# Differential attention: a head's output norm in steps among the next head's projections, with two buffers of attended values

## The reference

```python
def _diff_attend(q, k, v, lam):
    s = jnp.einsum('bqhte,bkhte->bhtqk', q, k).astype(jnp.float32) * (q.shape[-1] ** -0.5)
    p = jax.nn.softmax(s, axis=-1)
    a = (p[:, :, 0] - lam * p[:, :, 1]).astype(v.dtype)
    return jnp.einsum('bhqk,bkhe->bqhe', a, v)
...
    yb = _sweep_query_blocks(lambda n, qn: _diff_attend(qn, kb_all, vb_all, lam), qb)
    yb = rmsnorm(yb, b_subln_g) * (1.0 - lam_init)
    y = jnp.concatenate([ya.reshape(B, S, -1), yb.reshape(B, S, -1)], axis=-1) * jax.nn.silu(g)
    x = x + gate * (y @ w_out)
```

## Time and profile before

| what | us |
|---|---|
| median of 3 runs | 3795.56 |
| lowest, highest | 3795.41, 3795.64 |
| the profiled execution's own time | 3793.61 |
| its span, first to last instruction | 3791.6 |
| TensorE busy in the span | 3455.3 (91%) |
| VectorE busy | 2125.5 (56%) |
| ScalarE busy | 1412.0 (37%) |
| GpSimd busy | 298.5 (8%) |

### The profile page before, as it was taken

The page is one execution under the profiler, slowest core; times in us unless marked ns, Lnnn a source line. Parts: engine busy times, 40 slices in busy tenths (PEclk is TensorE's granted clock), DMA queues, the critical chain, the costliest instruction groups (busy, mean ns, idle before and its releaser), DMA issues. The chain is left out here.

```text
span 3791.6 us, 43707 instructions
## 1 busy us (share of the span) xinstructions
PE 3455.3 (91%) x17694; PEld 2681.2 (71%) x17694; DVE 2125.5 (56%) x3914; ACT 1412.0 (37%) x2577; POOL 298.5 (8%) x433
## 2 busy tenths in 40 slices
PE   6999988997998999999899988888799999988888
PEld 4777766664877888887765677777687666676677
DVE  5799954444757666565556554454355444334444
ACT  4222264444133222322333244444324555434441
POOL 2022110001102000000000000000001000000000
PEclk9899998998999999999999998998799999999999
DMA  3333320002522222332210100001212011010112
GB/s 133 111 124 133 139 85 24 23 30 105 190 90 67 81 84 84 111 131 81 84 31 25 49 23 30 23 30 37 97 57 74 30 37 33 23 35 7 35 51 88
DMA packets 76920, 258.21 MB, mean 68 GB/s; under 512 B 9960, under 2 KB 12008, under 8 KB 76720
## 3 DMA queue, kind: packets, MB, share of 16 engines
q1 hardware_dynamic: 42192, 132.68, 10.5%
q0 software_dynamic: 31072, 110.16, 8.5%
q10 hardware_dynamic: 3456, 12.58, 0.8%
HBM read 194.06 MB, written 50.85 MB: 65 GB/s over the span
## 5 line engine op out<-in xcount | busy, mean ns | idle before, releaser
L2878 PE MATMUL PS<-m,m 128*128 128x512 f32 (+3 forms) x3476 | 1394.3, 403 | 92.7 <-DVE m L3238 23.3
L2880 PE MATMUL PS<-m,m 128*128 128x512 f32 (+3 forms) x3476 | 1338.0, 386 | 0.0
L2879 PE MATMUL PS<-m,m 128*128 128x512 f32 (+3 forms) x3476 | 1338.0, 386 | 0.0
L2878 PEld LDWEIGHTS PS<-m,m 128*128 128x128 f32 (+2 forms) x3476 | 664.1, 192 | 325.7 <-issue 73.1
L2880 PEld LDWEIGHTS PS<-m,m 128*128 128x128 f32 (+2 forms) x3476 | 664.6, 192 | 133.7 <-issue 1.0
L2879 PEld LDWEIGHTS PS<-m,m 128*128 128x128 f32 (+2 forms) x3476 | 667.6, 193 | 119.5 <-issue 1.2
L3167 ACT COPY m<-PS 128x512 f32<-128x512 f32 x352 | 205.2, 588 | 451.0 <-PE PS L2994 450.1
L3004 PE MATMUL PS<-m,m 128*64 128x256 f32 (+1 forms) x1408 | 309.1, 411 | 28.3 <-ACT m L3167 21.1
L3238 DVE TENSOR_TENSOR m<-m,m 128x512 fp32r<-128x512 f32 (+4 forms) x299 | 233.2, 799 | 165.5 <-ACT m L3079 164.3
L3079 ACT CAST m<-m 128x512 fp32r<-128x512 f32 (+4 forms) x299 | 198.4, 697 | 335.0 <-DVE m L3452 182.9
L2985 PE MATMUL PS<-m,m 64*128 64x256 f32 (+5 forms) x1968 | 249.5, 363 | 47.4 <-ACT m L3156 28.0
(11 more groups left out here) (204 smaller groups left out, 3149.0 us busy)
## 6 DMA issues: line engine op xcount, KB each, us to landing
m<-in_w SPq DMA_DIRECT2D x222, 512.0 KB, 3.8
g_scratch<-m ACTq DMA_DIRECT2D x24, 512.0 KB, 2.6
m<-g_scratch POOLq DMA_DIRECT2D x24, 512.0 KB, 4.6
u_scratch<-m POOLq DMA_DIRECT2D x40, 256.0 KB, 3.2
m<-u_scratch POOLq DMA_DIRECT2D x20, 512.0 KB, 4.2
m<-in_w SPq DMA_DIRECT2D x40, 256.0 KB, 4.0
x_scratch<-m POOLq DMA_DIRECT2D x2, 4096.0 KB, 13.4
m<-m POOLq DMA_DIRECT2D x60, 128.0 KB, 2.7
```

Of the source, the lines that this page charges most:

```text
L2878: pe.e.engine.matmul(o, L[0], X[0], start=start, stop=False)
L2879: pe.e.engine.matmul(o, L[0], X[1], start=False, stop=False)
L2880: return pe.e.engine.matmul(o, L[1], X[0], start=False, stop=stop)
```

## The change

The norm of head h is no longer made in one piece at the start of head h + 1. A generator `norm_between` cuts it into steps, and `weave(..., norm, 8)` puts one step behind each 8 projection steps, that is at the end of a chunk, of the next head's q and k (in the last head: of the gate `eg7`). The squares of chunks 0 and 1 are made at the head's start; then the sums of 8 tiles, copied from PSUM to `inverse`, and the square of chunk 2; then silu, the sums of the last 2 tiles, and the root from SBUF; then one step per chunk with its broadcast and multiplies; then the store. There are two buffers of attended values (`yts`) and two for squares; the gate of the last head goes to `zq`. Line numbers of the engine programs are 49 higher in the kernel after.

```diff
-        def gate_steps(name, chunks, free, banks):
-            e_ = copy_to(lambda t0, tn: zg[:, t0:t0 + tn], after=free)
+        def gate_steps(name, chunks, free, banks, to=None):
+            z = to or zg
+            e_ = copy_to(lambda t0, tn: z[:, t0:t0 + tn], after=free)
...
+            yts = [yt, mem([P, TC])]
+            sq = [mem([P, 512]) for _ in range(2)]
+            yt_free, zgs = [[], []], [zg, zg, zg, zq]
...
+            def norm_between(h, free, banks):
+                y = yts[h % 2]
+                def square(c, after):
+                    t0, tn = CH2[c]
+                    n = p.id()
+                    p.add("square", n=n, x=y[:, t0:t0 + tn], q=sq[c % 2][:, 0:tn], r=None, after=after)
+                    return (S.square, n)
+                def sums_of(cs, after):
+                    b, n = take(banks), p.id()
...
+                    p.add("copy", n=m, d=inverse[:, 4 * cs[0]:4 * cs[0] + len(tiles)], o=o, scale=1.0, after=[(S.mean, n)])
+                    bank_free[b] = [(S.evac, m)]
+                    return n, m
+                sq_t = [square(c, list(free)) for c in range(2)]
+                yield
+                n, _ = sums_of((0, 1), sq_t)
+                sq_t = [square(2, [(S.mean, n)])]
+                yield
+                p.add("gsilu", n=h, z=zg[:, :], after=gate_done)
+                n, m = sums_of((2,), sq_t)
+                p.add("root", n=n, rs=inverse[:, :], ps=inverse[:, :], eps=None, free=[(S.evac, m)])
+                yield
+                for c, (t0, tn) in enumerate(CH2):
+                    b = take(banks)
+                    r, t = spread(b, (n, inverse, None, 1, False), t0 // 128, tn)
+                    p.add("subln", n=(h, c), y=y[:, t0:t0 + tn], g8=g8[:, 0:1], r=r, z=zg[:, t0:t0 + tn],
+                          after=[t, (S.gateact, h)])
+                    bank_free[b] = [(S.outd, ("norm", h, c))]
+                    yield
+                normed = (S.outd, ("sub", h, 2))
+                yt_free[h % 2] = [y_store(4 + h, y, TC, [normed])]
...
                 def steps():
+                    norm = norm_between(h - 1, ready, at.fill_banks) if h else iter(())
                     if h:
-                        yield from finish_steps(h - 1, ready, at.fill_banks)
+                        yield next(norm)
...
-                        yield from next_steps(CHE, qk, at.fill_banks)
+                        yield from weave(next_steps(CHE, qk, at.fill_banks), norm, 8)
...
-                        yield from gate_steps("eg7", CH2, done, at.fill_banks)
+                        yield from weave(gate_steps("eg7", CH2, done, at.fill_banks, zq), norm, 8)
...
-                                  "evac": (yt[:, 128 * b0:128 * b0 + 256], slice(0, P), None, y_free)})
+                                  "evac": (yts[h % 2][:, 128 * b0:128 * b0 + 256], slice(0, P), None, list(yt_free[h % 2]))})
...
-                at.run(units, list(begin), Fill(steps(), 11 + (76 if h < 3 else 52)), 11, tail,
+                at.run(units, list(begin), Fill(steps(), (11 if h else 3) + (76 if h < 3 else 52)), 4 if h else 3, tail,
```

More of the change, by code:

```diff
@@ L2422, in schedule @@
             p.add("gain8", out=g8[:, :], g=vc("subln"))
+            yts = [yt, mem([P, TC])]
+            sq = [mem([P, 512]) for _ in range(2)]
+            assert mem.at <= z_at
+            yt_free, zgs = [[], []], [zg, zg, zg, zq]
             stored, squares_done = [], {}
+            def norm_between(h, free, banks):
[7 more added lines that the diff above has]
+                    b, n = take(banks), p.id()
+                    tiles = [(c, i) for c in cs for i in range(CH2[c][1] // 128)]
+                    o = bank(b)[:, 0:len(tiles)]
+                    p.add("cols", n=n, parts=[(o[:, x:x + 1], [(sq[c % 2][:, 128 * i:128 * i + 128], cc("o128")[:, 0:1]),
+                                                               (ident, squares[h % 2][:, 4 * c + i:4 * c + i + 1])])
+                                              for x, (c, i) in enumerate(tiles)],
+                          after=after + [squares_done[h]], free=bank_free[b])
+                    m = p.id()
+                    p.add("copy", n=m, d=inverse[:, 4 * cs[0]:4 * cs[0] + len(tiles)], o=o, scale=1.0, after=[(S.mean, n)])
[18 more added lines that the diff above has]
+                normed = (S.outd, ("sub", h, 2))
+                zs_free.append(normed)
+                yt_free[h % 2] = [y_store(4 + h, y, TC, [normed])]
+                stored.extend(yt_free[h % 2])
+                p.add("ready", on="act", after=[normed])
+                yield
@@ L2436, in finish_steps @@
             def finish_steps(h, free, banks):
+                yt, zq, zg = yts[h % 2], zgs[0], zgs[h]
                 p.add("gsilu", n=h, z=zg[:, :], after=gate_done)
@@ L2452, in finish_steps @@
                 normed = (S.outd, ("sub", h, 2))
-                zs_free.append(normed)
-                y_free[:] = [y_store(4 + h, yt, TC, [normed]) if h < 3 else normed]
-                stored.extend(y_free)
-                p.add("ready", on="act", after=[normed])
+                y_free[:] = [normed]
             for h in range(4):
@@ L2510, in schedule @@
                 pass
-            t = split(Hh[:, 7, :], Hl[:, 7, :], yt[:, :], y_free)
+            t = split(Hh[:, 7, :], Hl[:, 7, :], yts[1][:, :], y_free)
             h_ready.update({(7, t0): t for t0, _ in CH2})
```

## The result

| what | before | after |
|---|---|---|
| median, us (13 runs each) | 3795.41 | 3804.59 |
| lowest, highest | 3788.29, 3799.88 | 3799.13, 3809.73 |
| profiled execution, span | 3793.61, 3791.6 | 3805.36, 3803.6 |
| loop of heads in the trace, from the first score block to the last of the last norm's sums | 529.1 | 537.9 |

The ratio is 1.0028 with a 95% interval of 1.002 to 1.0036: slower, by about 0.3%. The forecast was 3788.2 (3776 to 3803). Ahead of the loop and behind it the two traces differ by 1.1 and 2.0 us; the rest, 8.8, lies in the loop.

The account below looks back on a forecast made before the run. Bounds: the norm's one-bank string between the first score blocks; elsewhere TensorE, or an 8.6 us string per pair. Heads 1, 2, 3 and 0 give -2.4 - 2.4 - 0.6 - 2 = -7.4 from 3795.56: 3788.2, range 3776 to 3803.

Parts of the forecast that it names:

- the walk of the first five pairs: Head 1, pairs 1 to 5 step by step: 9.9, 15.4, 14.9, 13.7, 15.7, together 69.6 us against 69.25 before.
- the 1.1 behind them: Pairs behind pair 5: of 3.9 us of projection work done earlier, 1.1 lost where pairs 8 to 10 reach their lower bound.
- The clock's 2.5: Heads 1 to 3: lower TensorE clock around the sums, now among projections, gives back 2.5 us a head.
- the waits' 6.6: Heads 1 to 3: new waits among the norm's steps, pairs 3 to 5 included, give back 6.6 us a head.
- First stretch, second block, turns: Head 1 start: stretch 22.2 to 9.9 us, second score block at full clock -1.57, last turns and wait -1.0.
- Head 0: Smaller fill count moves 8 steps from pairs 1 to 8 into pairs 9 and 10: -2 us, between 0 and -3.
- Pair 3 and the price of a switch: Third pair 14.9 us, TensorE standing over 4; each table-set switch costs its load alone, 1.28, without a drain.
- the rival of dearer switches: Third pair, heads 1 to 3: each of three switches holds ScalarE another 1.28, 11.5 us more, 3799.7; chance 0.03.
- the clock's case: Rival: sums lower the clock as long as before, 8.4 us lost a head, 3805.9; sign head 1 clock 0.92; chance 0.17.
- Head 3: Last head with the moved norm: gains 17.0 us, gives back 16.4, sum -0.6.
- covered waits: Rival: new waits are hidden; heads 1 and 2 -5.2 and -6.5, head 3 -3, head 0 -2: 3778.9; chance 0.20.

Follow-up runs that it names:

- the second pair of traces: The kernel before and the changed kernel, each unaltered and traced a second time: loop of heads 525.9 us before, 534.3 us changed.

## Why the prediction was wrong

It gave 7.4 us less where the loop took 8.8 more: 16.2 apart (15.8 in the second pair of traces). Its sum for heads 1 and 2 rests on the walk of the first five pairs and on the 1.1 behind them. The clock's 2.5 and the waits' 6.6 only share out what the walk leaves, and the walk itself has about 1.9 for the clock.

- **First stretch, second block, turns**: right. 9.67, 10.82 and 9.67 for 9.9; the second block of head 1 at 2.01.
- **Head 0**: right, -2.0, and shown alone (-3.1 in the second pair of traces).
- **Pair 3 and the price of a switch**: right. 14.89 for 14.9, released by the copy of the sums and the exponentials; the rival of dearer switches is out, since each load begins within 0.02 of the end of what stands before it.
- **"The clock ... I take 2.5"**: wrong. Pair 2 alone lost 16.30 x 0.21 = 3.4, and with pairs 4, 6, 7 and 9 (1.7, 0.2, 1.5, 3.4) head 1 lost 10.3; before, the first two pairs lost 8.4 and 1.9. The clock's loss moved and did not shrink in this execution; in the second trace it was 7.0. Over head 1 the clock is 0.93, where the prediction gave 0.96 and named 0.92 as a sign of the clock's case: by that sign the case came true, but the runs put only pair 2's fall down to the sums. The prediction priced the fall behind the sums and none behind places where TensorE stands.
- **"Of the 3.9 saved behind pair 5, 1.1 is lost"**: the step that failed most. All 3.9 were lost and 2.8 more in head 1, and the same in head 2 (69.4 for 66.6): 5.6 above the forecast in each, 11 of the 16.2. In the second pair of traces it is 5.1 and 3.8, 9 of the 15.8. The prediction walked five pairs with the order in hand and gave the other five a flat price. Without any norm near them they take 69.1; the steps done earlier move the chunks' ends to where a copy holds the exponentials (1.87 in pair 8) or they hold it (2.47 in pair 6), and the fall in pair 9 comes with that. With the chunks' ends three pulls later they take 64.2 without the norm and 64.4 with it.
- **The walk of pairs 1 to 5**: 69.6 forecast, 71.5 measured, most of the difference clock in pairs 2 and 4. Pair 3's 14.9, to the hundredth, has a little luck in it: head 2's took 15.8 at a clock of 0.89.
- **Head 3**: -0.6 forecast. From its first block to the final norm's sums it took 134.4 for 131.9, so 2.4 more, and 5.4 more in the second pair of traces. Without the switches its nine pairs fall from 110.8 to 105.9, so the same string on ScalarE is probably most of it; as these nine pairs took 106.0, 102.7 and 103.1 in three traces without the change, a single trace can't show it. What else sets head 3 stays open.
- **The rivals**: covered waits, no. The clock's case came nearest in time (3805.9 for 3804.59), but without the sums the falls outside pair 2 stay or move.

## What to carry to other kernels

When steps are put among others that take turns at one buffer, walk the whole cycle and not the part where the new steps stand: what is done earlier shifts every later turn, and on an in-order engine a copy that changes places with a pair's exponentials cost 1.9 us one way and 2.5 the other here. Put a string of table switches where its engine idles already (here behind a pair's exponentials, for 9 us a head against 17, both with the chunks' ends three pulls later), and try the same program with a few empty steps before judging the idea, since two of them were worth 12 to 13 us a head here.

## What was not expected of the hardware

The lower of the two clock levels (1.2 GHz) came in pairs with no sums, near places where TensorE had stood. In heads 1 and 2 of all 17 traces, pair 9 goes with pair 8: where pair 8 stood for 2.5 to 2.9 us (16 heads of eight traces, the changed kernel's among them), pair 9 was at 0.68 to 0.83, and where pair 8 stood for 0.3 to 1.0 (18 heads of nine traces, the kernel before among them), pair 9 was at 1.00. Yet standing is not enough: pair 4 of the kernel before stands 2.5 in head 1 and pair 5 is at 1.00, both times that it was traced. What else decides is left open.
